# Two feed-forward blocks of a float32 kernel: another order of loads, column sums and weight roundings, the plain product last in the first block's down part, and x brought back in pieces

## The reference

```python
def conv_ffn(h, w_in, conv_w, conv_b, w_out):          # first block, D_FF = 2816
    u, v = jnp.split(h @ w_in, 2, axis=-1)
    u = causal_depthwise_conv_of_width_3(u, conv_w) + conv_b
    return (jax.nn.gelu(u, approximate=False) * v) @ w_out

# x = x + gt_f * conv_ffn(rmsnorm(x, g) * (1 + sc_f) + sh_f); then a norm, and the second block's
# mixer on [16 meta tokens, x]; then
# second block, width 4096:  x = h + rmsnorm(relu(rmsnorm(h) @ w_ff1) ** 2 @ w_ff2)
```

## Time and profile before

| | |
|---|---|
| median of three runs | 2378.28 us (2377.05 to 2380.7) |
| the profiled execution's own time | 2377.78 us |
| its span, first to last instruction | 2375.9 us |
| TensorE busy (matmuls) | 2209.5 us, 93% of the span |
| VectorE busy | 1781.1 us, 75% |
| ScalarE busy | 1136.8 us, 48% |
| GpSimd busy | 421.4 us, 18% |
| DMA | 276.38 MB, 116 GB/s on the mean |
| mean granted TensorE clock | 0.944 of full speed |

### The profile page before, as it was taken

The page is one execution under the profiler, slowest core; times in us unless marked ns, Lnnn a source line. Parts: engine busy times, 40 slices in busy tenths (PEclk is TensorE's granted clock), DMA queues, the critical chain, the costliest instruction groups (busy, mean ns, idle before and its releaser), DMA issues. The chain is left out here.

```text
span 2375.9 us, 31093 instructions
## 1 busy us (share of the span) xinstructions
PE 2209.5 (93%) x10909; PEld 1877.4 (79%) x10909; DVE 1781.1 (75%) x2931; ACT 1136.8 (48%) x1948; POOL 421.4 (18%) x418
## 2 busy tenths in 40 slices
PE   8989699998999999999999989789989999999996
PEld 5779688886887788887887979667878788788875
DVE  7699766665689987876789585573789987658797
ACT  5478655445353343334444563484553333554442
POOL 2122222222430122220001212003321111000002
PEclk9985599999999999999999999799999999999997
DMA  9014200004443332239431101002345534755431
GB/s 379 22 63 155 80 14 14 31 1 152 128 155 125 122 132 103 98 116 332 155 94 42 45 27 36 18 1 89 106 169 219 197 146 181 276 168 164 135 92 71
DMA packets 93097, 276.38 MB, mean 116 GB/s; under 512 B 11136, under 2 KB 15648, under 8 KB 89120
## 3 DMA queue, kind: packets, MB, share of 16 engines
q1 hardware_dynamic: 85472, 226.64, 28.5%
q10 hardware_dynamic: 7488, 47.98, 4.9%
HBM read 208.19 MB, written 66.39 MB: 116 GB/s over the span
## 5 line engine op out<-in xcount | busy, mean ns | idle before, releaser
L158 PE MATMUL banks<-f_hi,f_w_hi 128*128 128x512 f32 x608 | 238.0, 391 | 4.9 <-DVE f_w_lo L3884 3.6
L159 PE MATMUL banks<-f_lo,f_w_hi 128*128 128x512 f32 x608 | 237.2, 390 | 0.0
L160 PE MATMUL banks<-f_hi,f_w_lo 128*128 128x512 f32 x608 | 237.1, 390 | 0.0
L3415 ACT CAST f_w_hi<-f_raw 128x512 fp32r<-128x512 f32 x173 | 107.6, 623 | 256.0 <-PE banks L160 190.6
L1985 ACT CAST w_hi<-w_raw 128x512 fp32r<-128x512 f32 x152 | 94.1, 622 | 230.2 <-PE set L160 99.5
L158 PE MATMUL set<-gate_hi,w_hi 128*128 128x512 f32 x420 | 164.6, 392 | 4.0 <-issue 3.2
L159 PE MATMUL set<-gate_lo,w_hi 128*128 128x512 f32 x420 | 163.9, 390 | 0.0
L160 PE MATMUL set<-gate_hi,w_lo 128*128 128x512 f32 x420 | 163.9, 390 | 0.0
L158 PE MATMUL set<-b_hi,w_hi 128*128 128x512 f32 x384 | 150.9, 393 | 5.8 <-DVE w_lo L2315 5.8
L3095 POOL TENSOR_TENSOR f_w_lo<-f_raw,f_w_hi 128x512 fp32r<-128x512 f32 x64 | 95.1, 1488 | 335.3 <-ACT f_w_hi L3415 335.3
L160 PE MATMUL set<-b_hi,w_lo 128*128 128x512 f32 x384 | 150.4, 392 | 0.0
(11 more groups left out here) (577 smaller groups left out, 6129.7 us busy)
## 6 DMA issues: line engine op xcount, KB each, us to landing
gates<-x ACTq DMA_DIRECT2D x25, 1536.0 KB, 5.9
w_raw<-in_w_ff SPq DMA_DIRECT2D x53, 512.0 KB, 3.6
gate_raw<-gates SPq DMA_DIRECT2D x105, 256.0 KB, 2.8
f_gate_raw<-gates SPq DMA_DIRECT2D x70, 256.0 KB, 2.8
ada<-in_ada_w SPq DMA_DIRECT2D x32, 512.0 KB, 3.5
f_raw<-in_f_w_v SPq DMA_DIRECT2D x26, 512.0 KB, 3.5
f_raw<-in_f_w_u SPq DMA_DIRECT2D x25, 512.0 KB, 3.8
down_raw<-in_w_ff SPq DMA_DIRECT2D x18, 512.0 KB, 4.3
```

The costliest lines, as they stand in the source:

```text
L158: nc.tensor.matmul(out, w_hi, x_hi, start=start, stop=False)
L159: nc.tensor.matmul(out, w_hi, x_lo, start=False, stop=False)
L160: return nc.tensor.matmul(out, w_lo, x_hi, start=False, stop=stop)
L3415: nc.scalar.copy(w_parts(n)[0][:, :], source(n)).then_inc(w_hi_s, 1)
```

## The change

It has five parts. In the second block's down part x comes back in eight pieces, after b = 12, 14, ..., 26, and the last group's sixth weights after b = 29 and 31. At that part's start `sum_h(0)` moves to after unit 8, and ScalarE's and VectorE's lists there are reordered. In the first block's down part the order becomes P1, P2, P7, P6, P5, P3, P4; the loads of x, of weights and of mixer weights get other places; what VectorE does beside the last group follows the new order; and the mixer's first weights change buffers, the first being cast after u66 and the second after the first eight pieces of the last product.

The second block's down part, SyncE:

```diff
-DOWN_1 = (P1, P2, P7, P6, P4, P5, P3)
+DOWN_1 = (P1, P2, P7, P6, P5, P3, P4)
...
                     if b == 12:
                         for i in range(2):
                             sp.wait_ge(spilled[i], 16 * SPILLS * (PAIRS // 2) - (16 if i == LAST % 2 else 0))
-                        for k in range(KT):
-                            sp.dma_start(xs[:, k, META:META + T], d["x_keep"][k]).then_inc(back, 16)
-                        load_down(ENDS, 5, 0)
-                        load_down(ENDS, 5, 1)
+                    if 12 <= b < 12 + 2 * KT and b % 2 == 0:
+                        k = (b - 12) // 2
+                        sp.dma_start(xs[:, k, META:META + T], d["x_keep"][k]).then_inc(back, 16)
+                    if b in (29, 31):
+                        load_down(ENDS, 5, (b - 29) // 2)
```

The second block's start: TensorE, then ScalarE (`t4_high`, `t1_high` and `b22_high` are casts of input blocks, four of each), then VectorE:

```diff
                 for n in range(2, 2 * EARLY):
                     early_product(n, 0, HALF)
-                sum_h(0, acc[0])
+                    if n == 8:
+                        sum_h(0, acc[0])
...
                 weights_high(12)
                 early_out(9)
+                weights_high(13)
+                early_out(10)
                 for kk in range(HALF):
                     t4_high(kk)
-                weights_high(13)
-                early_out(10)
                 weights_high(14)
                 early_out(11)
-                for kk in range(HALF):
+                for kk in range(2):
                     t1_high(kk)
                 weights_high(15)
                 early_out(12)
+                for kk in range(2, HALF):
+                    t1_high(kk)
+                weights_high(16)
                 for kk in range(HALF):
                     b22_high(kk)
-                weights_high(16)
                 early_out(13)
...
+                weights_sum(16)
                 for kk in range(HALF):
                     t1_low(kk)
-                dve.wait_ge(h_total, 1)
-                for kk in range(2):
-                    b22_low(kk)
-                weights_sum(16)
-                for kk in range(2, HALF):
-                    b22_low(kk)
                 weights_low(16)
                 weights_sum(17)
+                dve.wait_ge(h_total, 1)
+                for kk in range(HALF):
+                    b22_low(kk)
+                weights_low(17)
+                weights_sum(18)
                 for kk in range(2):
                     part_low(P4, 8, kk)
-                weights_low(17)
-                weights_sum(18)
                 for kk in range(2, HALF):
                     part_low(P4, 8, kk)
                 weights_low(18)
```

The first block's down part, SyncE. Before, `bring_x(0)` to `bring_x(3)` stand after b = 4, 6, 12 and 14, `load_down(1, j)` for j = 0 to 5 after b = 5, 7, 8, 9, 10 and 11, and the two `load_mix` after b = 16 and 17:

```diff
+                BRING_AT = {5: 0, 11: 2, 14: 1, 24: 3}
+                DOWN_AT = {7: 0, 9: 1, 12: 2, 15: 3, 17: 4, 19: 5}
                 for b in range(4, len(units.down)):
                     load_gate(b)
+                    if b in BRING_AT:
+                        bring_x(BRING_AT[b])
+                    if b in DOWN_AT:
+                        j = DOWN_AT[b]
...
+                    if b in (26, 28):
+                        load_mix(b // 2 - 13)
```

TensorE (the first four pieces of `last_down`), then ScalarE, then GpSimd:

```diff
-                        pe.wait_ge(dve_sum, len(TOTAL_ORDER))
+                        pe.wait_ge(folded, folds_at(1, P3))
...
-                    if n == units.down_at(1, P4, 0):
+                    if n == units.down_at(1, P5, 0):
                         end_gate_high(0)
                         end_gate_high(1)
-                    if n == units.down_at(1, P4, 3):
+                    if n == units.down_at(1, P3, 3):
                         end_weights_high(0)
                         end_weights_high(1)
+                    if n == units.down_at(1, P4, 3):
+                        weights_mix(0)
...
-                weights_mix(0)
-                weights_mix(1)
                 meta_high()
                 for m in range(KT):
                     u_high(m)
+                weights_mix(1)
...
                 weights_mix(0)
-                weights_mix(1)
                 pool.wait_ge(added, 1)
                 for t in (z_hi, z_lo):
                     nc.gpsimd.memset(f32(t[:, :, META + T:T2]), 0.0).then_inc(padded, 1)
+                weights_mix(1)
```

More of the change, by code:

```diff
@@ L2696, in __init__ @@
         self.end_g_raw = [at(f"f_end_g_raw{j}", SLOT(3) + 4 * KB * j, [P, T]) for j in range(2)]
-        self.mw_hi = [at(f"mix_w_hi{i}", 8 * KB * i, [P, KT * P], F32R) for i in range(2)]
-        self.mw_lo = [at(f"mix_w_lo{i}", 8 * KB * i + 4 * KB, [P, KT * P], F32R) for i in range(2)]
+        self.mw_hi = [at(f"mix_w_hi{i}", 8 * KB * (1 - i), [P, KT * P], F32R) for i in range(2)]
+        self.mw_lo = [at(f"mix_w_lo{i}", 8 * KB * (1 - i) + 4 * KB, [P, KT * P], F32R) for i in range(2)]
         self.gw_hi = at("gates_hi", 16 * KB, [P, KT * P], F32R)
@@ L3040, in _ @@
                 low_done(sp, units.at[(MATS - 1, P4)])
+                BRING_AT = {5: 0, 11: 2, 14: 1, 24: 3}
+                DOWN_AT = {7: 0, 9: 1, 12: 2, 15: 3, 17: 4, 19: 5}
                 for b in range(4, len(units.down)):
                     load_gate(b)
-                    if b == 4:
-                        bring_x(0)
-                    if b == 5:
-                        for f in range(2):
[L3047 to L3062, removed]
+                    if b in BRING_AT:
+                        bring_x(BRING_AT[b])
+                    if b in DOWN_AT:
+                        j = DOWN_AT[b]
+                        if j in (1, 2):
+                            sp.wait_ge(done, UP)
+                        if j in (3, 4, 5):
+                            sp.wait_ge(conv_s, 4 * PAIRS)
+                        for f in range(2):
+                            load_down(1, j, f)
+                    if UP + b - 4 == units.down_at(0, P4, 0):
                         sp.wait_ge(dve_lo, units.low[UP + b - 4])
@@ L3288, in mix_products @@
                     if n == 0:
[L3289 removed]
+                        pe.wait_ge(folded, folds_at(1, P4))
                         pe.wait_ge(meta_dve, KT + 2)
@@ L3510, in end_gate_high @@
                     act.wait_ge(end_loaded, 64)
-                    act.wait_ge(dve_lo, units.low[units.down_at(0, P3, 2)])
+                    act.wait_ge(dve_lo, units.low[units.down_at(0, P4, 2)])
                     nc.scalar.copy(pl.end_g_hi[j][:, :], pl.end_g_raw[j][:, :]).then_inc(end_hi_s, 1)
@@ L3516, in end_weights_high, with weights_mix @@
                     nc.scalar.copy(pl.end_o_hi[h][:, :], pl.end_o_raw[h][:, :]).then_inc(end_hi_s, 1)
+                def weights_mix(n):
+                    act.wait_ge(m_loaded[n % 2], 16 * (n // 2) + 16)
+                    if n == 0:
+                        act.wait_ge(dve_lo, units.low[units.down_at(1, P4, 0)])
+                    elif n == 1:
+                        act.wait_ge(dve_lo, units.low[ALL - 1])
+                    else:
+                        act.wait_ge(m_done, n - 1)
+                    nc.scalar.copy(mw_hi[n % 2][:, :], mix_raw(n)).then_inc(m_hi_s, 1)
                 weights_wo(0)
@@ L3620, in meta_high @@
                     nc.scalar.copy(z_hi[:, :, 0:META], meta_back[:, :, :]).then_inc(meta_act, 1)
[L3622 to L3628, removed]
                 def u_high(m):
@@ L4037, in fold_set @@
                 def fold_set(q, i):
-                    a, first = {P2: (0, 0), P4: (0, HALF), P3: (1, 0)}[i]
+                    a, first = {P2: (0, 0), P3: (1, 0), P4: (0, HALF)}[i]
                     dve.wait_ge(back[2 * a + first // HALF], 16 * HALF)
@@ L4113, in last_group @@
                         dve.wait_ge(joined, 3)
-                        fold_total(P6, 1, 0, (0, 1), 28)
+                        fold_total(P6, 1, 0, (0, 1), 24)
                     elif (i, j) == (P3, 3):
-                        fold_total(P6, 1, 0, (2, 3), 28)
+                        fold_total(P6, 1, 0, (2, 3), 24)
                     elif (i, j) == (P3, 4):
                         join(3, P7, P5)
-                    elif (i, j) == (P3, 5):
+                    elif (i, j) == (P4, 0):
+                        fold_set(1, P3)
+                    elif (i, j) == (P4, 1):
                         dve.wait_ge(joined, 4)
                         fold_total(P7, 1, HALF, (0, 1), 32)
-                    elif (i, j) == (P3, 6):
+                    elif (i, j) == (P4, 2):
                         fold_total(P7, 1, HALF, (2, 3), 32)
+                    elif (i, j) in ((P4, 3), (P4, 4)):
+                        end_weights_low(j - 3)
                 nc.vector.scalar_tensor_tensor(c.gain[:, :], c.mod[:, SC_F:SC_F + 8], 1.0, c.col("g_ffn", 0, 8),
@@ L4222, in _ @@
                             last_group(i, j)
-                dve.wait_ge(folded, 36)
-                fold_set(1, P3)
+                fold_set(1, P4)
                 dve.wait_ge(folded, 40)
```

20 lines of the change are left out of this document (8 added, 12 removed).

## The result

The changed kernel took 2358.88 us (median of four runs, 2358.05 to 2361.94) against 2378.16 for the kernel before on the same chip: a ratio of 0.992, interval 0.9903 to 0.9937. The forecast was 2359.5. The profiled execution took 2358.05 us, its span is 2356.2, 19.7 less than before.

A forecast was written before the change was run, and what follows sets the result against it. TensorE, busy 93% of the span, was taken as the bound, so only its waits and slow clock mattered. Five terms, 6.5 - 3.4 + 4.8 + 6.4 + 4.4 = 18.7 us, took span 2375.9 to 2357.2, median 2359.5; eight-in-ten range 2350 to 2367.

The forecast's parts named there:

- Term 1: First block's down loads: SyncE's wait before bring_x(1) costs nothing and gate blocks go out on time, 6.5 us gained.
- Term 2: First block's last down steps: VectorE falls late in P5 and P3 and TensorE waits, 3.4 us lost.
- rival B: Small VectorE waits lower the clock (two times 1.7), unit 17's wait brings two slow stretches: 2364.6 us, chance 0.20.
- Term 3: End of the first block: the wait for last_add at the fifth piece and its slow stretch go, 4.8 us gained.
- 0.6 lost: Mixer's first product: the sixteenth u_low, held up by GpSimd's second mixer rounding, comes 0.6 us late.
- Term 4: Second feed-forward part's start: waits at units 13 and 16 go, unit 17 waits 2.9 us, 6.4 us gained.
- and that costs 1.7 more: Second part's start: a stretch at the lower clock follows unit 17's wait of 2.9 us, costing 1.7 us.
- the first of the two cases: Second part's start: GpSimd's rounding of 14 waits for one VectorE instruction at most; waiting out the run changes the sum by 1.2.
- Term 5: Second block's down part: x spread in pieces removes the late gate block after the load burst, 4.4 us gained.
- C: Loads in both blocks are late anyhow, so both load gains are 0: 2370.5 us, chance 0.05.
- D: Both spread load streams clog the queue, making the kernel slower: 2386 us at 220 GB/s, chance 0.03.
- A: ScalarE keeps up at the second part's start, 12.4 us gained there: 2353.5 us; 0.22 together with another case.

The follow-up runs named there:

- the one load moved: Kernel before, with only bring_x(1) moved to after b = 14 instead of b = 6: 2372.31 us, ratio 0.9974.
- squares late: Changed kernel, with early_out(15) directly after early_out(14) on ScalarE and the squares of x after it: 2361.19 us, ratio 0.9933 to the kernel before.
- the spread: Changed kernel, with VectorE's extra work beside the first block's last group spread over other steps, same instructions: 2355.16 us, ratio 0.991 to the kernel before.
- x in pieces alone: Kernel before, with only x brought back in eight pieces and the sixth weights later in the second block's down part: 2372.87 us, ratio 0.998.

## Why the prediction was right, term by term

The total is right within 1 us, and that is partly luck: two terms were off by 1.3 and 1.1, in opposite directions.

**Term 1, right, and so was its cause.** SyncE issued `bring_x(1)` at 1105.87 without a wait (near 1106 was forecast), and the one load moved brings 5.6 of 6.8. The small waits that I left 0.3 for do not exist.

**Term 2, right.** Forecast waits 0.16, 1.28, 1.28, 0.41, 0.49; the starts of u58, u59, u60, u61 and u63 came 0.19, 1.29, 1.29, 0.41 and 0.41 us more than 2.72 after the one before, and those of u62 and u64 0.13 more. (The view of waits calls the two long ones 1.0: from start to start such a wait costs 0.3 more than its gap.) No lower clock followed, so rival B's first half falls. The restarts, charged five times, came twice: the others lie in the waits themselves.

**Term 3, mis-sized: 3.5 instead of 4.8.** The last product behaves as forecast (21.76, no wait at the fifth piece). The 1.7 that the forecast charged to the old wait's slow stretch was no cost (above), but the 5.47 us are gained all the same: TensorE had to wait for VectorE with or without it. The step that failed is "0.6 lost" at the mixer's first product: it is 2.0. In the changed kernel (ScalarE, GpSimd, VectorE):

```profile
1290.65 1.03 ACT L3523 CAST mix_w_hi<-work 128x1024 fp32r<-128x1024 f32 x1
...
1291.76 2.48 POOL L3098 TENSOR_TENSOR mix_w_lo<-work,mix_w_hi 128x1024 fp32r<-128x1024 f32 x1 [10.83 <-ACT mix_w_hi L3523]
...
1291.88 0.74 DVE L4231 SCALAR_TENSOR_TENSOR x<-banks,mod,x 128x512 f32<-128x512 f32 x1
1293.47 1.32 DVE L4241 SCALAR_TENSOR_TENSOR z_lo<-x,f_gain_u,z_hi 128x512 fp32r<-128x512 f32 x1 [0.85 <-ACT z_hi L3634]
```

I counted only that GpSimd holds VectorE. It did, by 0.6 (1.32 instead of 0.74); but ScalarE's cast of 1.03 us and the squares queued behind it stand ahead of the next `u_high` too, and VectorE waited 0.85 for that. VectorE's pair of instructions takes 1.32 of 1.36 us per piece, so nothing of this is made up. The last `u_low` came 26.7 us after the last down unit, where I had 26.1 and 25.5 was needed, and the second wait, for the sums, follows from the first. Moving the pair ahead of the pieces gave back all 2.0.

The trace shows here which instruction is held: `last_add`, whose operands are a PSUM bank and one SBUF tile, took its usual 0.74 beside GpSimd, `u_low`, with two SBUF tiles, did not. The Trainium skill (SBUF — State Buffer, "Who interferes with whom") says this: an instruction of VectorE with at most one SBUF input, outside the modes that use two ports, does not contend with GpSimd. The trace agrees.

**Term 4, mis-sized: 7.5 instead of 6.4.** The mechanism is the one forecast: the waits of 4.1 and 4.0 go, unit 17 waits 2.6 for `early_out(15)` (2.9 forecast). The step that failed is "and that costs 1.7 more": no stretch at the lower clock followed, in any of the five profiles with this wait and this start. What I had not forecast is the 1.0 given back over the following units, and small waits of 0.5 and 0.1 at units 15 and 16. GpSimd's rounding of 14 did not wait out VectorE's run: it took 1.70 us, the longest of that line in the changed kernel 1.85. So the first of the two cases that I weighed held at this place. As a rule, "waits for one instruction at most" does not hold: at 1268.40 the mixer's rounding waited out a run of VectorE and took 5.67.

**Term 5, right.** No wait from b = 12 to 31.

Of the rivals, C and D are refuted by the two runs that change only loads (6.8 and 4.6 gained). A needed `early_out(15)` on time; moved alone (squares late) it gave nothing, and only with VectorE's list changed too did the start gain 10.9 of A's 12.4 us, 1.1 of which was given back. What B and the forecast shared, 1.7 us for each wait of 2.5 and more, was wrong in both places where the experiments could test it.

## What to carry to other kernels

- A queue that stands for one semaphore holds all that is behind it: moving one load past its wait gave 5.6 of 6.8 us, spreading the rest 1.1. Look for the one wait first.
- Count an engine's lateness unit by unit, each extra against its slack (here 2.72 us less 1.2 or 1.8). The count forecast waits of 0.2 to 1.3 us to a tenth, and told where to put the same instructions so that, with the mixer's first weights moved too, 3.9 us of waits vanish.
- The engine named by a wait may be only the last of several that are late together. Before moving its work, follow the next one (VectorE, 0.8 behind) and what waits for the moved work (a load behind the squares). And a rounding put beside a chain with 0.04 us of slack per step costs every engine's share of it, not GpSimd's alone.

## What the runs showed of the hardware that I had not expected

- The length of a wait alone did not decide whether the granted clock fell. Waits of 2.6 us at unit 17 were followed by a clock of 1.00 in five profiles out of five. Those of 2.6 to 3.0 in the second block's down part were followed by a stretch at 1.2 GHz in all five profiles that have one. One and the same wait went both ways: the 2.5 in the first block's up part was followed by such a stretch in 11 of 13 profiles (not in the spread and in x in pieces alone), the old end's 3.5 in four of five. What else decides, these runs do not show.
- A stretch at 1.2 GHz can be free: with the old end, last product and mixer's first products took 53.96 us with one and 54.28 without, since VectorE, and not TensorE, set the time. A longer one (6.8 us at 1.2 GHz instead of 3.4) was not: 55.18.
- GpSimd and VectorE hold each other up in both directions: the same rounding of 128x1024 took 2.48 and 2.65 us, or 5.67, and the same two `fold_total` 1.41 or 3.54. The one that loses can lose to several instructions in a row.
